# Asking for the up and down weights of one expert together in a mixture-of-experts decoder kernel

## What is computed

```python
def swiglu(x, w1, w3, w2):
    return (jax.nn.silu(x @ w1) * (x @ w3)) @ w2
# moe(): route, sort the tokens by expert, pad to blocks, then for each block
y = swiglu(x_pad[tok], w1[e], w3[e], w2[e])      # w1, w3: 1024 x 256, w2: 256 x 1024
acc.at[tok].add(y * wt[:, None])
out = acc[:T] + swiglu(xt, ws1, ws3, ws2)        # the shared expert, all tokens
```

## The kernel before

| load | first used by job | J: job that frees its slot |
|---|---|---|
| 17 | 18 | 15 |
| 18 | 18 | 16 |
| 19 | 19 | 16 |
| 20 | 19 | 17 |
| 21 | 20 | 18 |
| 22 | 20 | 18 |
| 23 | 21 | 19 |

## Time and profile before

### The profile page before, as it was taken

How to read it: one execution, slowest core, us unless ns; L and a number is a source line. 1 busy time by engine, 2 the same in 40 slices (tenths; PEclk the granted TensorE clock), 3 DMA queues, 4 the chain that set the end, 5 groups by cost and what they waited for, 6 DMA issues and landing times. The chain is left out here.

```text
span 2841.5 us, 37339 instructions
## 1 busy us (share of the span) xinstructions
PE 2567.9 (90%) x13849; PEld 1402.0 (49%) x13850; DVE 1037.1 (36%) x2342; ACT 669.8 (24%) x1452; POOL 335.4 (12%) x390
## 2 busy tenths in 40 slices
PE   6989989899989999989975999999899998999994
PEld 3665656656754433333332566576774443333331
DVE  3443343443353222312226445444444222222216
ACT  1031130312211222222212333433211222222221
POOL 0101001010000111111100122121101111111110
PEclk9999999999999999999997999999899999999997
DMA  7615235152426999999974021120624899999976
GB/s 270 183 57 159 78 109 164 52 185 87 184 90 243 347 419 407 402 395 403 397 285 169 30 89 54 64 74 30 217 112 181 333 399 400 394 397 411 397 284 266
DMA packets 177811, 654.90 MB, mean 230 GB/s; under 512 B 26884, under 2 KB 88684, under 8 KB 122504
## 3 DMA queue, kind: packets, MB, share of 16 engines
q1 hardware_dynamic: 130320, 522.82, 47.2%
q0 software_dynamic: 35136, 109.10, 10.9%
q10 hardware_dynamic: 12216, 21.19, 2.6%
HBM read 614.18 MB, written 53.52 MB: 235 GB/s over the span
## 5 line engine op out<-in xcount | busy, mean ns | idle before, releaser
L1430 DVE TENSOR_SCALAR core_oT<-moe_tx,moe_by,moe_plus 128x128 f32<-128x128 f32 x360 | 123.1, 405 | 725.9 <-PE moe_tx L1677 725.9
L1709 PE MATMUL moe_ph<-weights_w,core_oT 128*32 128x512 f32 (+2 forms) x1632 | 359.0, 631 | 25.1 <-issue 25.1
L675 PE MATMUL attn_proj<-core_hT,core_ring 128*128 128x512 f32 x768 | 341.4, 606 | 8.5 <-ACTq L497 5.1
L1728 PE MATMUL moe_py<-weights_w,moe_hT 128*32 128x512 f32 (+2 forms) x1312 | 312.6, 596 | 2.5 <-ACT moe_hT L1167 2.5
L1709 PE MATMUL moe_pr<-weights_w,core_oT 128*64 128x512 f32 (+2 forms) x992 | 279.6, 611 | 18.9 <-issue 18.9
L675 PEld LDWEIGHTS attn_proj<-core_hT,core_ring 128*128 128x128 f32 x768 | 149.1, 195 | 193.3 <-issue 187.5
L2327 PE MATMUL gdn_pj<-core_hT,core_ring 128*128 128x512 f32 x512 | 226.4, 597 | 0.0
L1167 ACT COPY moe_hT<-moe_th 128x256 f32<-128x256 f32 x98 | 36.6, 373 | 773.8 <-PE moe_th L1665 773.8
L1243 POOL DMA_INDIRECT y_rows<-moe_ysb,moe_yidx x90 | 91.7, 1019 | 974.7 <-ACT moe_ysb L1183 915.9
L1709 PEld LDWEIGHTS moe_ph<-weights_w,core_oT 128*32 128x32 f32 (+2 forms) x1632 | 109.1, 127 | 190.2 <-issue 189.7
L1709 PE MATMUL moe_ph<-core_ring,core_oT 128*32 128x512 f32 (+1 forms) x544 | 167.0, 640 | 14.5 <-issue 14.5
(11 more groups left out here) (394 smaller groups left out, 3284.0 us busy)
## 6 DMA issues: line engine op xcount, KB each, us to landing
weights_w<-in_expert_w_dram SPq DMA_DIRECT2D x294, 1024.0 KB, 12.8
core_ring<-in_expert_w_dram SPq DMA_DIRECT2D x90, 1024.0 KB
core_ring<-in_attn_w_in_dram SPq DMA_DIRECT2D x36, 1024.0 KB, 7.4
weights_w<-y_rows SPq DMA_DIRECT2D x32, 1024.0 KB, 12.8
attn_ada_w<-in_ada_w_dram POOLq DMA_DIRECT2D x64, 384.0 KB, 6.0
core_ring<-in_gdn_w_in_dram SPq DMA_DIRECT2D x16, 1024.0 KB, 6.0
attn_swp<-attn_raw ACTq DMA_DIRECT2D x192, 64.0 KB, 2.1
gdn_ada_w<-in_ada_w_dram POOLq DMA_DIRECT2D x32, 384.0 KB, 3.6
```

The costliest lines, as they stand in the source:

```text
L675: last = nc.tensor.matmul(proj[n % 2][:], w[:, j % SLOTS, kk, half_ * P:(half_ + 1) * P], c.hT[:, kk, :], start=kk == 0, stop=kk == KT - 1)
L1430: last = nc.vector.tensor_scalar(xT[:, b, k], tx[1][:, k - 4], by[:, k:k + 1], plus[:, k:k + 1], ALU.mult, ALU.add)
L1709: last = nc.tensor.matmul(ph[b][at, :], rows_t(k), w13[slot][:, :, k], start=k == 0, stop=k == KT - 1)
L1728: last = nc.tensor.matmul(py[n][at, :], hT2[:, b, k, at], w2[slot][:, k, half(n)], start=k == 0, stop=k == 1)
```

## The change

In the loop of SP over the loads 3 to 63, `load_down(n)` moves from behind `load_up(n+1)` to right behind `load_up(n)`. The variable that carried the postponed load goes. Number, size and destination of the DMAs, and every wait, stay as they are; only the order in SP's program changes, from up(n), down(n-1), up(n+1), down(n) to up(n), down(n), up(n+1), down(n+1).

```diff
-            waiting = None
             for n in range(ew.EARLY, NE):
                 e = expert(n)
                 freed = load_up(n, e)
-                if waiting is not None:
-                    load_down(*waiting)
-                waiting = n, e, freed
-            load_down(*waiting)
+                load_down(n, e, freed)
             sp.wait_ge(y_done, JOBS)
```

## The result

The kernel after the change takes 3026.26 us (median; 3014.07 to 3034.72), the kernel before 2834.51 in the same comparison: 1.0666 times as long, interval 1.0629 to 1.0703. The forecast was 3022. The execution that was profiled took 3034.2 us with a span of 3032.6, against 2841.5: 191.1 us more.

The account below looks back on a forecast made before the run. PE waits for up weights in the expert passes, DMA engines 98 to 99% busy. A period: 73.0 + 12 + 6 + 2 + 5 = 98.0 us against 81.75; with 13 at load 13, both layers 188 us: 3022, range 2936 to 3086.

Parts of the forecast that it names:

- The added wait: On SP, up(n+1) stands behind down(n), hence is issued at y(J_n); later up loads and PE wait too.
- Who holds SP: SP's queue before: mostly waiting in front of a down load, 314.2 us against 126.6, with the next up load behind.
- (a): Load 22, first used by job 20: PE waits a whole 3 MB trip from a dry queue, 12 us a period.
- (b): Loads 19 and 20, first used by job 19: 6 MB released together at y(16), PE waits 6 us a period.
- (c): Loads 18 and 24, one down and one up load per pass: waits of 2 us together, 0 to 4.
- The clock: Up matmuls behind the two long waits of a period run slow at 1.2 GHz: 5 us, 2.8 to 5.8.
- slower, much: Rival: clock stays low a whole pass behind each wait of 10 us or more; 3158 us, chance 0.08.
- Ahead of the first period: Before load 13, up loads have a pass or more to spare and DMA engines idle time: delay costs 0.
- J_(n+1) stood two jobs past J_n somewhere: Sign in the order of loads and jobs that would make the whole prediction wrong; no size given.
- The bytes decide: Rival: DMA engines, 98 to 99% busy, set a period's length whatever the order; 2834 us, chance 0.03.
- a fuller rate: Rival: faster, transfers at 422 to 426 GB/s instead of 400 over a period; 2788 us, chance 0.02.
- Slower, but little: Rival: the 6 MB group lands in time and the clock recovers within the wait; 2878 us, chance 0.07.

Follow-up runs that it names:

- the run with a sixteenth: Kernel after the change, loading from load 7 on only a sixteenth of each row of the down weights (64 KB an expert instead of 1 MB): 2954.44 us.
- the first run: Kernel before, with only the down load's wait for y(J_n) taken ahead of the next up load, DMAs in the old order: 2956.2 us.
- the third run: Kernel before, with the change made for all loads except 12, 21, 30, 39, 48 and 57: 2896.78 us.
- the last experiment: Kernel before, with down(n) issued behind up(n+2) and a fifth up slot: 2817.47 us, 0.9932 times before.

## Why the prediction was right, step by step

*The added wait.* Right, and shown from both sides: the wait alone costs 121 us, and a fifth down slot, which makes the same wait harmless, gives all of the 192 us back. The step that said "at y(J_n)" reads off the timeline: down(21) at 2480.11, up(22) 1.46 us behind.

*Who holds SP.* The reading behind the theory was right in its direction, but it set 314.2 us for down loads against 126.6 for up loads and left out the 55.5 us of the `moe_pr` line: the up loads had 182.1.

*(a) 12 us a period.* Measured in layer 1: 11.03 to 12.87, mean 11.8 in the five periods (11.7 with the one at job 14). The bounds were 9.8 and 14.0. Its parts hold too: 2.5 us for the megabyte in front, against 2.3 in the run with a sixteenth and 2.2 to 2.6 in the first run, less the issue. The Trainium skill's figure for one DMA (page "DMA: Bandwidth & Descriptors", section "Anatomy of one DMA — SWDGE (gpsimd) path") gave an estimate of 9.2 us for the 3 MB. From the issue of the down load to PE's start the six trips took 11.5 to 13.3 us, mean 12.2. Here the row was the better guide, and 2988 us would have been 38 us too low. The rule of the Trainium skill (same page, section "Rules for kernel authors") to issue early and wait late is borne out: issuing the same loads later, in the same order, cost 121 us.

*(b) 6 us.* Measured 1.60, 3.43, 2.29, 6.49 and 5.53: mean 3.9, so the term was too large by 2. It is the difference of two times, and both were off. The 6 MB group took 20.5 to 21.5 us from the issue of its first load, at y(16) or its like, to PE's start, where the forecast had 17.2 to 19.8. But PE was ready for job 19 or its like only 15.0 to 19.2 us after that issue, where the forecast had 12.9, since wait (c) at job 18 and the slow matmuls behind it lie between the two. In the first period the group's first load is issued at 2447.22, job 18 waits until 2451.43, and PE is ready for job 19 at 2466.46. Period by period, (b) is short where (c) is long: 1.6 to 3.4 us behind waits of 3.4 to 3.8, and 5.5 to 6.5 behind 2.4. Where (c) is gone, in the kernel after with half of the down weights, (b) is 5.5 to 7.2 us, mean 6.2, although its group is 1 MB smaller. The prediction added (b) and (c) as if they were independent.

*(c) 2 us for two passes together.* Measured 2.4 to 3.8 in one pass, the one that load 18 serves, and none in the other: mean 3.2. Right in its bounds, too small by 1. (b) and (c) together are 7.0 against 8.

*The clock, 5 us.* PE is busy 78.0 us in a period (the mean of the four windows above), 5.0 over the floor of 73.0, as forecast. The three waits are 11.8 + 3.9 + 3.2 = 18.9 us, and 0.7 us are short waits for row indices, which the sum didn't have. The forecast took a longer wait to cost no more than a short one, and that is what the rows show. Behind place (a), two windows:

```profile
2484.50:2498.20 13.70, 4.76 (x24) 1.35 (x28) 0.00 (x0) 0.00 (x0) 0.00 (x0) 0.50 1.00 393
2498.20:2508.00 9.80, 9.80 (x77) 3.76 (x71) 2.93 (x11) 2.29 (x7) 0.00 (x0) 1.00 0.14 58
```

PE is granted 0.50, the 1.2 GHz level, for 13.7 us, far longer than the 5.7 us of the earlier trace rows; but it does nothing for 8.9 of them, and its matmuls are slow for 4.8 us only, which costs 2.4. The rival "slower, much", a whole pass at the lower clock, falls with this.

*Sum.* 98.0 forecast and 97.6 measured for a period, 112 and 107.9 us for the waits of a layer, 188 and 192 for the whole. That (b) was too large by 2 while (c) and the left-out waits were too small by 2 is luck: the mechanism and (a) were right, but a hit to 0.4 us is closer than the terms were. The DMA share was forecast as 0.82 and is 0.83 to 0.88, mean 0.86; by rate it fits, 339 GB/s against the 335 that 400 x 82/98 gives.

*Ahead of the first period.* The cost was put at 0 before load 13, and in layer 1 PE has no wait of over 0.3 us for up weights before job 14. "J_(n+1) stood two jobs past J_n somewhere" was named as a sign of being wrong for the whole. By the kernel's own tables it is so twice, for loads 3 and 4 and for loads 10 and 11. Both lie in this stretch, so the sign was drawn too wide.

*The rivals.* "The bytes decide" and "a fuller rate" fall with the result itself: the same bytes take 192 us longer. What is true of the second is seen in the last experiment: 407 to 420 GB/s over a period is to be had, but by letting up loads out earlier. "Slower, but little" had the longer wait of (a) give (b) room. The runs don't bear that out: with (a) taken out, the third run, (b) is 2.4 to 7.3 us, mean 4.6, no longer than 6. In the traces it is (c) that gives it room; no run takes (c) alone away.

*The down loads gain nothing.* Right: no wait of PE for a down load in front of L1728 before or L1724 after.

## What to carry to other kernels

A queue that issues in order carries its waits to everything behind them: one wait moved forward cost 121 us here. Ask of each load not only when it is needed, but when its slot comes free, and sort by the second: a load with slack whose wait ends late belongs behind the urgent ones, or needs a slot more. Which of two buffers should get the room is read from the line on which the issuing engine waits, not from the data that arrive late.

## What was not expected of the hardware

Half of a load saved nothing in the kernel after: with 0.5 MB of 1 MB, in rows of 4 KB, the long waits had a mean of 12.1 us against 11.7, with the DMA engines busy 0.81 of a trip instead of 0.92. In the kernel before the same cut gave 45 us. Loading 64 of 128 rows, half of the bytes again, made the kernel 221 us slower. Only a sixteenth of each row brought what the bytes are worth.

The transfers into a dry queue are not at full rate at once. In the first 3.0 us of the trip the kernel after moves 188 to 197 GB/s at the five places of kind (a) from job 14 to job 38, in the next 3.5 us 311 to 414, and in the rest 402 to 413. For the first 1.1 to 1.5 us only the 1 MB of the down load is in the queue. The 311 belong to job 20, the longest of the trips. Two windows of it:

```profile
2481.60:2484.60 3.00, 0.00 (x0) 0.00 (x0) 0.00 (x0) 0.00 (x0) 2.02 (x2) 0.99 1.04 360
2484.60:2487.00 2.40, 0.00 (x0) 0.00 (x0) 0.00 (x0) 0.00 (x0) 0.00 (x0) 0.50 0.80 253
```

253 GB/s for 2.4 us in the middle of this trip, with every compute engine idle. What slows it isn't shown by any run here.
